# Feed-forward pairs: two block products of the next tile ahead of the down outputs

## The reference

```python
h = _rmsnorm(x, norm_ffn_g[l])
gt, up = jnp.split(h @ w_gate_up[l], 2, axis=-1)     # w_gate_up: 1024 x 2*2816
x = x + (jax.nn.silu(gt) * up) @ w_down[l]           # w_down: 2816 x 1024
return _rmsnorm(x, final_norm_g)
```

## Time and profile before

| what | value |
|---|---|
| runs of the kernel before | 1944.6, 1947.63, 1948.3 us (median 1947.63) |
| the profiled execution, its own time | 1945.05 us |
| its span | 1943.0 us |
| TensorE matmul busy | 1884.4 us, 97% |
| VectorE busy | 1150.8 us, 59% |
| ScalarE busy | 815.8 us, 42% |
| GpSimd busy | 252.1 us, 13% |
| mean granted TensorE clock | 0.991 of full speed |
| feed-forward pairs 1 to 10 (down outputs of pair 0 to those of pair 10) | 1301.4 to 1908.8 us of the span |

### The profile page before, as it was taken

The page is one execution under the profiler, slowest core; times in us unless marked ns, Lnnn a source line. Parts: engine busy times, 40 slices in busy tenths (PEclk is TensorE's granted clock), DMA queues, the critical chain, the costliest instruction groups (busy, mean ns, idle before and its releaser), DMA issues. The chain is left out here.

```text
span 1943.0 us, 27344 instructions
## 1 busy us (share of the span) xinstructions
PE 1884.4 (97%) x9286; PEld 1580.8 (81%) x9286; DVE 1150.8 (59%) x2167; ACT 815.8 (42%) x1519; POOL 252.1 (13%) x259
## 2 busy tenths in 40 slices
PE   6999999999999998999999999999999999999997
PEld 3888888888888887888888887777888888888886
DVE  5466766656676777224332237698567665676655
ACT  5556556666776666224331121443223322233223
POOL 2311111111111100000000000012121221212211
PEclk9999999999999999999999999999999999999998
DMA  8422222222222212213112122102111211112112
GB/s 239 127 72 76 66 78 68 80 58 65 81 61 80 79 44 83 59 48 92 42 45 71 49 83 102 48 22 66 58 50 43 65 43 57 51 43 65 43 44 98
DMA packets 145232, 133.24 MB, mean 69 GB/s; under 512 B 7316, under 2 KB 130324, under 8 KB 142856
## 3 DMA queue, kind: packets, MB, share of 16 engines
q1 hardware_dynamic: 142936, 131.77, 22.8%
q10 hardware_dynamic: 2224, 0.56, 0.1%
HBM read 109.17 MB, written 16.06 MB: 64 GB/s over the span
## 5 line engine op out<-in xcount | busy, mean ns | idle before, releaser
L196 PE MATMUL ps<-h_hi,w_hi 128*128 128x512 f32 x1104 | 446.1, 404 | 6.2 <-DVE h_lo L2011 2.9
L198 PE MATMUL ps<-h_hi,w_lo 128*128 128x512 f32 x1104 | 433.0, 392 | 0.0
L197 PE MATMUL ps<-h_lo,w_hi 128*128 128x512 f32 x1104 | 432.1, 391 | 0.0
L196 PEld LDWEIGHTS ps<-h_hi,w_hi 128*128 128x128 f32 x1104 | 208.6, 189 | 47.9 <-DVE h_lo L2011 3.6
L198 PEld LDWEIGHTS ps<-h_hi,w_lo 128*128 128x128 f32 x1104 | 208.3, 189 | 45.9
L197 PEld LDWEIGHTS ps<-h_lo,w_hi 128*128 128x128 f32 x1104 | 208.6, 189 | 37.8
L1980 DVE TENSOR_TENSOR residual<-residual,ps 128x512 f32<-128x512 f32 x240 | 162.3, 685 | 118.1 <-PE ps L198 109.8
L752 POOL TENSOR_TENSOR w_lo<-w_raw,w_hi 128x256 fp32r<-128x256 f32 x138 | 102.0, 770 | 550.6 <-ACT w_hi L779 515.4
L1881 ACT ACTIVATE w_hi<-bias 128x512 fp32r<-128x512 f32 x60 | 38.0, 633 | 295.5 <-POOL bias L1764 220.4
L1764 POOL TENSOR_TENSOR bias<-w_raw 128x512 f32<-128x512 f32 x20 | 26.1, 1304 | 997.3 <-DVE act_lo L1994 573.6
L196 PE MATMUL ps<-w_down_hi,act_hi 128*128 128x512 f32 x352 | 137.0, 389 | 0.3 <-issue 0.3
(11 more groups left out here) (287 smaller groups left out, 3835.1 us busy)
## 6 DMA issues: line engine op xcount, KB each, us to landing
w_raw<-in_w_in SPq DMA_DIRECT2D x60, 512.0 KB, 3.8
w_raw<-in_w_gate_up SPq DMA_DIRECT2D x44, 512.0 KB, 3.7
k_stack<-k_stack SPq DMA_DIRECT2D x24, 512.0 KB, 5.5
w_down_raw<-in_w_down SPq DMA_DIRECT2D x11, 1024.0 KB, 4.9
x_all<-in_x SPq DMA_DIRECT2D x8, 512.0 KB, 8.5
bias<-bias_a_scratch SPq DMA_DIRECT2D x4, 1024.0 KB, 6.0
heads_bc_scratch<-heads_out SPq DMA_DIRECT2D x8, 512.0 KB, 2.9
bias<-neg_c_scratch SPq DMA_DIRECT2D x4, 1024.0 KB, 5.1
```

The lines of the kernel that those rows point to most:

```text
L196: nc.tensor.matmul(out, w_hi, x_hi, start=first, stop=False)
L197: nc.tensor.matmul(out, w_hi, x_lo, start=False, stop=False)
L198: return nc.tensor.matmul(out, w_lo, x_hi, start=False, stop=last)
```

## The change

TensorE makes SUM_1 of a pair's first tile also ahead of the down outputs of the pair in front, and not behind them. So that the weights are there in pair 1, VectorE splits that block of pair 1 ahead of the first additions, and not after the fourth. Everything else is as it was.

```diff
@@ block_ffn, VectorE, ahead of the loop over pairs @@
             dve.sem_inc(joined, 2 * JOINS - GATE0_DONE)
             dve.wait_ge(hid_lo, 4)
+            w_low(1, 0, SUM_1)
             group = OUT_GROUPS
             add_group(group, range(0, 2))
             dve.wait_ge(t_sums, T3_AT[1])
             for part in range(T_PARTS):
                 t_lo(t3, t3_sum, 2, part)
             add_group(group, range(2, 4))
-            w_low(1, 0, SUM_1)
             add_group(group, range(4, 6))
@@ block_ffn, TensorE @@
             def pair_body(i, last):
-                tile(i, 0, [GATE_A])
+                tile(i, 0, [GATE_A, SUM_1])
                 pair_down(i)
-                tile(i, 0, range(SUM_1, PRODUCTS))
+                tile(i, 0, range(SUM_2, PRODUCTS))
                 tile(i, 1, range(PRODUCTS))
```

## The result

The changed kernel takes 1955.67 us (median of five runs, 1955.28 to 1958.06); the kernel before, in five runs beside it, 1947.63 (1942.78 to 1948.3). The ratio is 1.0053, with a 95% interval of 1.0040 to 1.0066: 10.3 us slower, between 7.8 and 12.9. Against the 1945.05 us from which the sum was made, I had forecast 6.8; against the median of 1947.63 the forecast time of 1951.8 us was only 4.2 more. The new median lies in the range I gave, but the loss was half as large again as my sum.

The account below looks back on a forecast made before the run. TensorE, busy 1884.4 of 1943.0 us, was taken as the bound. Pair 1's shift 4.9, boundaries 1.1, new clock fall 1.7 and old fall -0.9 sum to 6.8 us; on 1945.05 that gives 1951.8 us, range 1948.0 to 1957.0.

Parts of the forecast that it names:

- The cover, 0 us: Down outputs begin one product, 2.72 us, later; with no wait there to remove, the added cover gains 0 us.
- The chain of the later pairs stays: Later pairs: the VectorE and ScalarE chain to the second tile's UP_B gets no shorter, so its waits, 6.4 us, stay.
- Boundaries, 0.13 x 8 = 1.1 us: Pairs 3 to 10: SUM_1 meets the SUM_4 read just ending and restarts late, 1.1 us in all (0 to 2.0).
- SUM_1 of pair 1 waits 4.2 us: Pair 1: TensorE waits 4.2 us (3.2 to 4.2) for the low part of SUM_1, split beside GpSimd's third sum.
- A fall of the clock behind it, +1.7: Pair 1, after the 4.2 us pause: one fall to TensorE's lower clock for 3.4 us, costing 1.7 us (0 to 3.4).
- Out of that go 0.6 us for the moved split, and 1.1 us of the t3 splits ... 4.4 to 5.4 us: 4.9: Pair 1: VectorE's 30.96 us up to the SUM_3 read shrinks by these savings; first tile's UP_B starts 4.9 us later.
- the 0.5 us that I had taken off: Pair 1: half of the 1 us saved before UP_B if VectorE's 1.77 us split comes free of GpSimd.
- The fall at 1356, -0.9: Pair 1: the existing slow clock after the 2.08 us pause may go or stay, -1.8 or 0; taken as -0.9 us.
- the shift stays to the end: Pair 1 after the first tile's UP_B: an unchanged VectorE and ScalarE chain carries the 4.9 us delay to the end.

Follow-up runs that it names:

- e9: Kernel before, old order, with VectorE reading SUM_4 ahead of the low split of the first half's hidden values: 1942.91 us, ratio 0.9996 to the kernel before.
- e6: Kernel before, old order, with the down weights split during each pair's first tile, in idle times: 1936.29 us, ratio 0.9962 to the kernel before.
- e1: Changed kernel with pair 1 back in the old order, pairs 2 to 10 in the new: 1944.67 us, ratio 1.0007 to the kernel before.
- e0: The changed kernel unaltered, timed again: 1954.4 us, ratio 1.0057 to the kernel before.
- e4: Changed kernel, but in pair 1 GpSimd's third sum waits until VectorE has split SUM_1's weights: 1954.12 us in one run.
- e3: Changed kernel with VectorE's t3 splits and pair 1's SUM_2 and SUM_3 weight splits ahead of the first addition: 1953.25 us, ratio 1.0055 to the kernel before.
- e7: Changed kernel, new order, with the down weights split during each pair's first tile: 1946.75 us, ratio 1.0020 to the kernel before.
- e10: Changed kernel with VectorE's prologue t3 splits, weight splits and t4 sums among or ahead of the first eight additions: 1949.71 us, ratio 1.0033 to the kernel before.
- e8: Changed kernel with pair 1 in the old order and VectorE reading SUM_4 ahead of the first half's low split: 1941.2 us, ratio 0.9990 to the kernel before.

## Why the prediction was right in sign and short in size

By its own steps, from the trace after:

**The cover, 0 us.** Right. At all ten beginnings before, the second down matmul follows the first at 0.22 to 0.23 us, so there was no loss to be bought off, and e9 shows at most 0.06 us even with a later split.

**The chain of the later pairs stays.** Right: eight waits at UP_B as before, 0.41 to 0.82 us. e6 shows the link that I had not priced, the down splits.

**Boundaries, 0.13 x 8 = 1.1 us.** Right in kind, a little small. From SUM_1's place to the first down output the nine boundaries of the changed kernel take 0.14 to 0.25 us more than the 2.72 of a product, 1.8 us together; pair 2's, which I had put at 0, is one of them, since its read came no earlier there. e1's later pairs are 0.10 us longer than those of before and e0's 0.11; the profiled run of the changed kernel had 0.26, of which 0.06 each are waits at UP_B that differ from run to run.

**SUM_1 of pair 1 waits 4.2 us.** Right: 4.25 us behind its place, with the split held up by GpSimd's third sum, which e4 took away. **A fall of the clock behind it, +1.7.** Right: the down outputs begin 8.7 us later than before, 7.1 + 1.7 were forecast.

**"Out of that go 0.6 us for the moved split, and 1.1 us of the t3 splits ... 4.4 to 5.4 us: 4.9".** This is the step that failed. With the clock's 1.7 us UP_B of the first tile should have come 6.6 us late, and it came 9.4 us late (42.1 us behind the place, 32.7 before). I took the work between VectorE's first addition and the SUM_3 read as one block, from which each saving comes off in full. The stretch from the first addition to the SUM_3 read became 31.8 us and not 31.0, where I had subtracted 1.7 and half of 1.0: 3.0 us more than my sum. This has two halves of about 1.5 us.

The first half: the savings were not had. Ten additions stand in the block that cannot come before TensorE's outputs. The ninth and the tenth in the kernel before:

```profile
1314.91 1.27 DVE L1980 TENSOR_TENSOR residual<-residual,ps 128x512 f32<-128x512 f32 x2
```

The tenth starts at about 1315.5, 14.1 us behind the first down matmul; after the change, where VectorE waits for the output, it starts 13.8 us behind it (1327.19 for 1313.39). So only 0.3 us could be saved up to there, whatever was taken out, and the savings turned into 0.67 + 0.23 + 0.23 us of new waiting for TensorE. e3 shows it: with more work moved from ahead of the tenth addition, UP_B comes no earlier.

The other half: I let GpSimd cost less behind the tenth addition, and it cost more. The t4 splits took 3.96 us and not 2.85, one step of the t4 sums 1.72 and not 1.21, while another weight split met nothing and took 0.68 and not 1.23; that is 1.1 us more, and the 0.5 us that I had taken off did not come, as the split of 1.77 us took 1.75.

**The fall at 1356, -0.9.** It went: the way from UP_B of the second tile to pair 2 is 8.35 us and not 9.92. And the pause ahead of it went too, which I had not forecast: "the shift stays to the end" was wrong by 1 us. The d_lo splits met GpSimd less (3.44 us for 4.54), and TensorE, slowed by the new fall, came there late. The two gave back 2.6 us of the 9.4, so that the traces differ by 6.9 in pair 1. What the new fall at UP_B of the first tile cost is open: in e7, whose down splits are out of the way, TensorE takes 20.6 us from there to UP_B of the second tile with a fall, and the changed kernel takes 20.7, with VectorE's read ending just in time; e10, without a fall, takes 19.6.

**The terms against the trace.** The forecast was 4.9 + 1.1 + 1.7 - 0.9 = 6.8. The trace has 7.7 for UP_B of the first tile, 1.7 for the clock, 2.2 for the later pairs, -1.6 for the fall that went and -1.0 for the pause that went: 9.0 us, the 9.1 of the stretches but for rounding.

**What stood against the base.** The second thing that was mis-sized is the base itself. I added the sum to the profiled execution of the kernel before, 1945.05 us, and left the 2.6 us up to its median to the range. That execution's pair 1 was a long one: 64.3 us, with the pause of 2.08 us and the slow clock, against 61.5 us in e1 and 61.3 in e8, which have the same order in pair 1, with a pause of 0.9 us and no fall, and 62.3 us in e9, with 2.07 us of pause and no fall. And for each of the eleven kernels of the table that have an interval, the runs put the kernel further up against the kernel before than its stretch against the 607.4 us does, by 1.3 to 4.2 us, in the middle 3.1. A base stretch some 3 us longer than in a usual execution would explain all eleven at once, and the step from 9.1 us in the traces to 10.3 and 11.1 in the runs with them. It is an inference: there is no second profile of the kernel before.

## What to carry to other kernels

A product moved ahead of a block of other work needs its operands earlier by the length of the whole block, in the first iteration too, where they come from a prologue with an order of its own; look there first, since 7 us of this loss in the trace, and 9 in the runs, lay in one pair of ten. When a chain on another engine is interleaved with outputs of the engine that you delay, do not shift it as a block: find the last output that it has to wait for; what is saved ahead of it counts only up to the time at which that output is there. And before adding cover to a wait, see that the wait is there: here it was at UP_B, and moving two weight splits into idle time was worth 7.4 us in the order of before.

## What the runs showed of the hardware

- A read that ends just ahead of the place of the product that waits for it still costs: the second matmul follows at 0.33 to 0.34 us and not 0.227, at eight of the nine boundaries of the changed kernel (at the ninth it starts 0.13 us late and follows at 0.30), and nothing of it is listed as a wait. With the split that is waited for 0.2 us ahead, as in e9, the second matmul follows at 0.23 to 0.29 us, a loss of 0.06 us at most.
- A fall of TensorE's clock to its lower level (1.2 of 2.4 GHz, for 3 to 3.5 us) followed every pause of 3.1 us or more in pair 1, in all eight profiles that have such a pause; of the pauses of about 2.1 us at UP_B, one was followed by a fall and one, in e9, was not: pair 1 took 64.3 and 62.3 us. The pause of about 2 us ahead of pair 0, the same in every kernel here, was followed by a fall in the profiles of e3, e8 and e9 and by none in the other ten. So after 2 us the same code falls in one execution and not in the next.
- VectorE's 128x512 splits of two SBUF inputs cost 1.16 to 1.78 us instead of 0.69 when a GpSimd sum was running as they began, and ended 0.53 to 0.56 us behind the end of that sum, wherever in it they began. So it is in all 218 rows of a single weight split in pairs 1 to 10 that begin inside a sum, in the thirteen profiles. One wait that lets VectorE go first brought the 0.69 back, and GpSimd lost 0.86 us by it.
